# Six attentions of a two-block network: values stationary in two column tiles, outputs split from PSUM, probabilities divided by VectorE before they are transposed

## The reference

```python
# first block, even mixer ("swa"): 8 query heads on 2 key/value heads, window 127, a sink logit a head
p = exp(s - m);  l = sum(p) + exp(sink - m);  o = (p @ v) / l
x = x + concatenate([conv_branch(h), o], -1) @ w_out
# first block, odd mixer ("dil"): 8 heads, three dilated windows merged, so each key counts mult(distance) times
p = mult * exp(s - m);  l = sum(p);  o = (p @ v) / l
x = x + concatenate([o, pool_branch(h)], -1) @ w_out
# second block, twice: "dsa" (4 heads, keys chosen by a top-64 of index scores) and "mla" (4 heads, width 96)
p = softmax(where(allowed, s, NEG));  o = p @ v
merged = sum(gates[n] * (branch[n] @ w_branch[n]));  x = x + merged @ w_out
```

## Time and profile before

| | us |
|---|---|
| median of 3 runs | 1781.18 |
| all runs | 1781.18, 1781.10, 1785.13 |
| the profiled execution | 1784.89 |
| its span in the profile | 1783.1 |
| PE busy | 1768.1 (99%) |
| PE weight loads busy | 1500.8 (84%) |
| DVE busy | 1246.4 (70%) |
| ACT busy | 935.2 (52%) |
| mean granted PE clock, share of full speed | 0.998 |

### The profile page before, as it was taken

How to read it: one execution, slowest core, us unless ns; L and a number is a source line. 1 busy time by engine, 2 the same in 40 slices (tenths; PEclk the granted TensorE clock), 3 DMA queues, 4 the chain that set the end, 5 groups by cost and what they waited for, 6 DMA issues and landing times.

```text
span 1783.1 us, 25102 instructions
## 1 busy us (share of the span) xinstructions
PE 1768.1 (99%) x9850; PEld 1500.8 (84%) x9850; DVE 1246.4 (70%) x1839; ACT 935.2 (52%) x1304; POOL 30.5 (2%) x41
## 2 busy tenths in 40 slices
PE   9999999999999999999999999999999999999998
PEld 8888878888888888888888788888888888888887
DVE  7776645876587657677656977777756878677774
ACT  6554545554455446555545545455544544555553
POOL 0000100000000001000000000000000000000000
PEclk9999999999999999999999999999999999999999
DMA  8666643666666655466656544566666454466663
GB/s 270 199 179 201 179 135 119 191 182 207 184 193 179 201 173 178 121 195 184 195 175 178 173 131 132 179 184 189 190 191 174 143 154 127 149 191 189 188 195 109
DMA packets 231294, 312.26 MB, mean 175 GB/s; under 512 B 23614, under 2 KB 179934, under 8 KB 231178
## 3 DMA queue, kind: packets, MB, share of 16 engines
q1 hardware_dynamic: 231014, 310.35, 57.8%
q10 hardware_dynamic: 164, 0.30, 0.1%
HBM read 308.91 MB, written 1.64 MB: 174 GB/s over the span
## 4 chain that ended last, share of the span: by engine, by line
PE 95%; DVE 3%; ACT 1%; issue 1%; DMA 0%; SPq 0%; POOL 0%; POOLq 0%; ACTq 0%
PE ps L654 26%; PE ps L603 16%; PE ps L605 16%; PE ps L604 16%; PE ps L656 13%; PE ps L1152 1%; PE ps L615 1%; DVE wlo L1734 1%; PE ps L836 1%; PE ps L862 1%; PE ps L849 1%; PE ps L804 1%; DVE m_scr L1743 0%; PE ps L899 0%; DVE m_scr L2383 0%
## 5 line engine op out<-in xcount | busy, mean ns | idle before, releaser
L1734 DVE TENSOR_TENSOR wlo<-staging,whi 128x1024 fp32r<-128x1024 f32 (+1 forms) x580 | 692.5, 1211 | 345.1 <-ACT whi L1250 344.9
L1250 ACT ACTIVATE whi<-staging 128x1024 fp32r<-128x1024 f32 (+1 forms) x580 | 606.4, 1050 | 486.9 <-PE ps L605 305.0
L654 PE MATMUL ps<-hT,whi 128*128 128x512 f32 x1984 | 623.7, 396 | 0.6 <-DVE wlo L1734 0.6
L656 PEld LDWEIGHTS ps<-hT,wlo 128*128 128x128 f32 x1984 | 372.7, 188 | 88.1
L656 PE MATMUL ps<-hT,wlo 128*128 128x256 f32 x1984 | 389.9, 278 | 0.0
L654 PEld LDWEIGHTS ps<-hT,whi 128*128 128x128 f32 x1984 | 302.1, 189 | 0.9 <-DVE wlo L1734 0.8
L603 PE MATMUL ps<-whi,fh 128*128 128x512 f32 x504 | 196.1, 389 | 0.0
L604 PE MATMUL ps<-wlo,fh 128*128 128x512 f32 x504 | 196.1, 389 | 0.0
L605 PE MATMUL ps<-whi,fl 128*128 128x512 f32 x504 | 196.1, 389 | 0.0
L603 PE MATMUL ps<-whi,hT 128*128 128x512 f32 (+3 forms) x464 | 184.5, 398 | 0.8 <-DVE wlo L1734 0.6
L605 PE MATMUL ps<-whi,hT 128*128 128x512 f32 (+3 forms) x464 | 177.4, 382 | 0.0
(11 more groups left out here) (350 smaller groups left out, 1856.4 us busy)
## 6 DMA issues: line engine op xcount, KB each, us to landing
staging<-in_w_in SPq DMA_DIRECT2D x92, 512.0 KB, 3.6
staging<-in_ffn_w_gate SPq DMA_DIRECT2D x84, 512.0 KB, 4.3
staging<-in_ffn_w_up SPq DMA_DIRECT2D x84, 512.0 KB, 4.5
staging<-in_ffn_w_down SPq DMA_DIRECT2D x84, 512.0 KB, 4.1
staging<-in_w_ffn_gate SPq DMA_DIRECT2D x44, 512.0 KB, 4.1
staging<-in_w_ffn_up SPq DMA_DIRECT2D x44, 512.0 KB, 4.5
staging<-in_w_ffn_down SPq DMA_DIRECT2D x44, 512.0 KB, 4.3
staging<-in_od_w_in SPq DMA_DIRECT2D x16, 512.0 KB, 3.6
```

What stands on the lines that cost most here:

```text
L654: e.matmul(o, wh[:, kk, j * 128:j * 128 + 128], hT[:, k, :], start=k == 0, stop=False)
L656: m = e.matmul(o[:, 0:256], wl[:, kk, j * 128:j * 128 + 128], hTh[:, k, :], start=False, stop=k == KD - 1)
L1250: e.activation(high(u)[:, 0:n], stage[u % NS][:, 0:n], ACT.Copy).then_inc(*K.inc("hi", ("hi", u)))
L1734: e.tensor_tensor(low_of(u)[:, 0:n], stage[u % NS][:, 0:n], high(u)[:, 0:n].bitcast(F32), ALU.subtract).then_inc(*K.inc("lo", ("lo", u)))
```

## The change

The groups alternate between the query tiles (`self.groups`: head pair by head pair, tile 0 then tile 1). A value product has the values stationary (128 x 64) and the transposed probabilities streaming (128 x 128); the two heads of a pair write partitions 0 to 63 and 64 to 127, so the output of a pair comes out already transposed, both query tiles in one bank. ACT writes the high part and DVE the low part straight from there; the buffers for the outputs, the output transposes and what followed them go. Since queries now lie along the columns, the division can't be done on the outputs: DVE takes the reciprocal of each group's sums and multiplies the probabilities, before they are transposed. In `swa` the sink's term is made for each group. The pairs of `swa` consist of two heads of different key/value heads, so the rows of `ev_w_out` are loaded in halves to fit.

```diff
             for c in (0, 256):
                 plan_cols(ev, c, 256)
                 plan_cols(ev, 512 + c, 256)
-            for r in (512, 768, 0, 256):
-                plan_rows(A["ev_w_out"][0], [r, r + 128])
+            for r in (512, 576, 640, 704):
+                w = A["ev_w_out"][0]
+                plan.append(([(0, w[r + c:r + c + 64, :], (1, 1024)) for c in (0, 256)], 1024))
+            plan_rows(A["ev_w_out"][0], [0, 128, 256, 384])
...
+                self.late, self.light, self.last = late, light, last
+                self.groups = [(t, h0) for h0 in range(0, H, 2) for t in range(2)]
...
-                self.rows = [(self.mh[:, 4 + k, :], self.ml[:, 4 + k, :], ("swa oT", k // 2))
+                self.rows = [(self.mh[:, 4 + k, :], self.ml[:, 4 + k, :], ("swa oT", k))
...
@@ tensor_program @@
             def attend(a):
...
                         t, h0 = groups[i]
-                        if h0 == 0:
-                            ops[t] = room((P + " o", t))
+                        if t == 0:
+                            ops[h0] = room((P + " o", h0))
                         e.wait_ge(*K.at(P + " pt", i))
-                        for j in range(2):
-                            for kt in range(t + 1):
+                        for kt in range(t + 1):
+                            for j in range(2):
                                 o = (j * (t + 1) + kt) * 128
-                                w = e.matmul(ops[t][:, (h0 + j) * 64:(h0 + j) * 64 + 64], a.pt[i % 2][:, o:o + 128],
-                                             a.vN(kt, h0 + j), start=kt == 0, stop=kt == t)
+                                w = e.matmul(ops[h0][64 * j:64 * j + 64, 128 * t:128 * t + 128], a.vN(kt, h0 + j),
+                                             a.pt[i % 2][:, o:o + 128], start=kt == 0, stop=kt == t)
                         w.then_inc(*K.inc("att", (P + " pv", i)))
-                        if h0 == H - 2:
-                            done(P + " o", t)
+                        if t:
+                            done(P + " o", h0)
...
-                        e.wait_ge(*K.at(P + (" ex" if a.mult is None else " pm"), i))
+                        e.wait_ge(*K.at(P + " light", i))
...
                     e.wait_ge(*K.at("ev k T", 0))
                     yield from attend(m.at)
-                    transposed("swa", m.o, 4)
...
@@ scalar_program @@
             def attend(a):
...
-                        if h0 == H - 2 and a.sink is not None:
-                            l = a.mx[:, 3, 8 * t:8 * t + H]
-                            e.wait_ge(*K.at(P + " sink in", t))
-                            e.activation(l, l, ACT.Exp).then_inc(*K.inc("exp", (P + " sink", t)))
+                        if a.sink is not None:
+                            l = a.mx[:, 3, c0:c0 + 2]
+                            e.wait_ge(*K.at(P + " sink in", i))
+                            e.activation(l, l, ACT.Exp).then_inc(*K.inc("exp", (P + " sink", i)))
+                    if 0 <= turn - 3 < H and groups[turn - 3][0]:
+                        k = groups[turn - 3][1] // 2
+                        hi, _, at = a.out
+                        e.wait_ge(*K.at(P + " pv", turn - 3))
+                        e.activation(hi[:, at + k, :], bk(P + " o", 2 * k)[:, 0:256], ACT.Copy).then_inc(
+                            *K.inc("oT", (P + " oT hi", k)))
...
@@ vector_program @@
             def attend(a, between=lambda turn: None):
...
+                def low(i):
+                    k = groups[i][1] // 2
+                    hi, lo, at = a.out
+                    e.wait_ge(*K.at(P + " oT hi", k))
+                    e.tensor_tensor(lo[:, at + k, :], bk(P + " o", 2 * k)[:, 0:256], hi[:, at + k, :].bitcast(F32),
+                                    ALU.subtract).then_inc(
+                        *K.inc("oTl", (P + " oT", k), ("ev", (P + " o", 2 * k)), *(a.last if i == H - 1 else ())))
+
                 for turn in range(H + 3):
-                    if 0 <= turn - 2 < H and groups[turn - 2][1] == H - 2:
...
+                    if 0 <= turn - 4 and groups[turn - 4][0]:
+                        low(turn - 4)
+                    if 0 <= turn - 1 < H:
                         i = turn - 1
                         t, h0 = groups[i]
                         nk, c0 = 128 * (t + 1), t * 8 + h0
+                        l, r = mx[:, 2, c0:c0 + 2], mx[:, 3, c0:c0 + 2]
+                        p = a.sm[i % 3][:, :, 0:nk]
                         e.wait_ge(*K.at(P + " ex", i))
...
+                        if a.sink is not None:
+                            e.wait_ge(*K.at(P + " sink", i))
+                            e.tensor_tensor(l, l, r, ALU.add).then_inc(*K.inc("att_sum"))
+                            e.wait_ge(*K.now("att_sum"))
+                        e.reciprocal(r, l).then_inc(*K.inc("att_sum", (P + " one by", i)))
+                        if a.light == "dve":
+                            e.wait_ge(*K.now("att_sum"))
+                            e.tensor_tensor(p, p, r.unsqueeze(2).broadcast_to([128, 2, nk]), ALU.mult).then_inc(
+                                *K.inc("light_dve", (P + " light", i)))
                     between(turn)
...
+                low(H - 1)
```

## The result

| | before | after |
|---|---|---|
| median of 4 runs each, us | 1782.96 | 1791.59 |
| all runs | 1781.18, 1781.10, 1785.13, 1784.74 | 1791.60, 1791.58, 1792.67, 1791.22 |
| the profiled execution | 1784.89 | 1791.60 |
| its span | 1783.1 | 1789.8 |

A forecast was written before the change was run, and what follows sets the result against it. PE, busy 99% of the span, bounds the kernel; other engines count only where PE waits. Terms 3.2 + 2.8 + 0.2 - 2.2 = 4.0 us more, giving 1785.2 us from a median of 1781.18; range 1777.5 to 1791.5.

The forecast's parts named there:

- The clock stays at 1.00 outside 268 to 276: Expected sign: granted clock falls only at the stretch already in the old profile (0.50 in 269 to 270).
- rival B: Both mixers: the granted clock falls in a new wait of PE, price 3.3 us, total 1788.5; chance 0.15.
- Odd mixer up to the pool: Divisions of groups 0 to 2 and larger early masks on DVE delay the pool matmuls: 3.2 us lost.
- Odd mixer after the pool: From turn 5 of dil, PE's values wait for DVE's low part in a shared output bank: 2.8 us lost.
- The loop: Dil after the pool: ACT copy and exp, DVE multiplicities, division, mask, low part; 5.3 us from a transpose's end.
- Even mixer: Divisions delay the shifted copies 1.5 us, values gain 1.5, two late waits lose 1.4; stated net 0.2 lost.
- Second mixers: Dsa and mla: transposes gain 1.7, values gain 3.7, shape changes lose 3.2, division covered; net 2.2 us gained.
- the pitch of 0.058: Value products in two column tiles: 0.058 us a record, taken from the convolution's taps, against 0.105 now.
- the change of shape: Switching between column-tiled value products and other matmuls: 0.20 us lost a group, 3.2 in the second mixers.
- Rival A: Value products: column tiles don't overlap, second mixers 3.7 us more, dil and swa about 1; total 1789.9; chance 0.10.
- Rival C: DVE keeps up in dil after the pool, and even-mixer exp doesn't delay copies: 1780.9; chance 0.20.
- rival D: DVE's cover holds everywhere, so PE's savings come through, 4.4 us gained plus about 1: 1775.8; chance 0.10.

The follow-up runs named there:

- e1: Changed kernel without the division (reciprocal and multiply) in dil, the odd mixer's attention: 1786.06 us; odd mixer +1.4 us over the kernel before.
- e4: Kernel before, with only dil's probabilities divided on DVE ahead of their transposes: 1789.06 us; odd mixer +4.6 us.
- e2: Changed kernel with groups in the old order and one output bank per query tile: 1788.15 us, ratio 1.0025 to the kernel before.
- e5: Changed kernel with filler matmuls of zeros on PE ahead of the bank waits in turns 5 and 7 of dil: span 1790.3 us, odd mixer +6.7.
- e7: Changed kernel with the two value matmuls of one head issued back to back: span 1789.2 us; eight value records still 0.59 us.
- e8: Changed kernel with the division's multiply done twice in the second mixers: span 1793.4 us; second mixers +3.2 us over the kernel before.
- e10: e7 with both heads of a pair in one column tile in the second mixers: span 1794.3 us; second mixers +3.2 over the kernel before.
- e11: Changed kernel without reciprocal and division in the second mixers' attentions: span 1789.5 us; second mixers -1.7 us against the kernel before.
- e6: Changed kernel with dil's division multiply on ACT, reciprocal left on DVE: span 1786.7 us; odd mixer +4.2 us over the kernel before.
- e9: Changed kernel with DVE taking dil's low part ahead of the next group's mask: span 1785.2 us; odd mixer +4.8 over the kernel before.

## Why the prediction was right or wrong

**Direction and range** were right, the size short by 2.7 us of 6.7: 1.5 are the fall of the clock in dil, 0.5 the even mixer, 0.5 the second mixers and 0.3 the part ahead of them, less 0.1 in the rest of the odd mixer. The step that failed is the one on the clock, "The clock stays at 1.00 outside 268 to 276"; the sum had nothing for a fall. A fall in a new wait of PE stood as rival B with a chance of 0.15 and a price of 3.3. That B's time, 1788.5, nearly is the 1788.7 measured is luck, since the fall cost half of that price and the rest came from elsewhere.

**Odd mixer up to the pool.** Right: 3.2 forecast, 3.0 measured. Of its parts the divisions were 1.9 to 2.0 rather than 2.4 (e1, e4) and the larger early groups 1.1 rather than 0.8 (e1, and 1.0 in e2). The transposes of group 1 stood at 706.83, 705.9 plus the 1.0 of the shift.

**Odd mixer after the pool.** 2.8 forecast, 4.4 measured, and 2.9 once the fall's 1.5 are taken off. The loop was laid out well: turn 5 at 721.51 (forecast 720.9 and 1.0 of shift), turn 7 at 729.72 (729.1 and 1.0), both behind DVE's low part. Turn 10 came at 740.67 where 738.2 and 1.0 were due, 1.5 late: the fall lies between. The wait for the bank is one place where DVE's lateness appears; e4 and e2 show that without it the same time goes at the division.

**The clock.** It fell once in dil in all six kernels that keep the changed order with the division on DVE as it stands (the changed one, e5, e7, e8, e10, e11), at 708, 722, 723 or 730, and in e2; never in e1, e4, e6, e9, nor where dil is as before. Each fall in dil began within 2 us of the end of a wait of PE for DVE. I had priced it at 3.3, from a stretch which by its loss (3.4) was as long as two of these, and against it I held the one wait of 1.84 us before the taps, which left the clock up. That was one sample, and e4 has the other: its even mixer is that of the kernel before, PE waits 2.31 us at the same place, the clock reads 0.73 in 252 to 253 and 0.50 behind it, and the taps take 4.48 us rather than 2.80:

```profile
251.82 4.48 PE L899 MATMUL ps<-ev_u,ev_w 128*32 128x256 f32 x48 [2.31 <-DMA ev_u<-ev_shift]
```

With the new `swa` it is the same: e5 and e7 lost 1.7 within 247 to 251, behind waits of 1.6 and 0.6 us that the changed kernel has too, without a fall there. What decides which wait brings it down is open: e6 has waits of 1.8 and 1.5 us in dil, e9 of 1.9 and 1.5, and neither a fall. That waits are needed for it is supported, and not shown, by e1 and e4, whose waits in dil are at most 1.3 us and which have no fall there, one trace each; e5 doesn't add to it.

**Even mixer.** 0.2 forecast, +0.7 measured, within -2 to +3. The 0.2 isn't what the prediction's own terms give: 1.5 for the copies and 1.4 for two waits, less 1.5 gained, are 1.4. Of the parts, the gate multiply came at 242.25 rather than 240.10, and the taps at 252.32 rather than 250.84, 1.5 later or 1.2 from the start of the stage. The waits for the low part's bank and the convolution's sums in the last turns were 0.37 and 0.49 us rather than 1.4, and the larger new waits stand ahead of the taps: 1.60 for the division and 0.56 for a low part, which use up the old wait for the copies (1.84 before, 0.17 now). From one kernel to another the stage moves by 1.0 to 1.7 us with a fall more or less, so the half microsecond isn't to be explained.

**Second mixers.** 2.2 forecast, 1.7 measured, and the terms close. Removed transposes: 16 x 0.109 = 1.7. Values: 8 x (0.84 - 0.59) + 8 x (0.39 - 0.37) = 2.2. What follows them: 16 x 0.14 = 2.2 lost, 12 times at transposes and 4 times at the first product behind the last group. In my terms: the pitch of 0.058 was right (0.055), and what goes with a group, 0.05 and 0.20, was 0.29 (0.15 ahead, in a four-record group of 0.37 = 0.15 + 4 x 0.055, and 0.14 behind). The term that was mis-sized is the change of shape, by 0.04 a group, 0.6 in all. So the column tiles by themselves gave nothing here; what was gained is the output transposes that they made needless. The 0.14 doesn't come from the overlap: with one column tile (e10) the transposes take 0.59 all the same.

Rival A is excluded by e10: without overlap the second mixers would be 4.9 us longer. By the rule of the Trainium skill (TensorE: Matmul & The Clock Gate, Part 3, What overlaps and what doesn't), a weight load runs beside matmuls in flight only when the row group differs, and both tiles here have the same rows. The traces disagree, and the measurement decides: a record costs 0.11 us in one tile, as much as its stream alone, and 0.055 in two, so load and stream of one tile run beside those of the other. The same page of the Trainium skill (Part 3, Measured speedup vs the span model) gives a speedup of 2.38 for three column tiles; two tiles here gave 1.02/0.59 = 1.7, which agrees in kind. Rival C is refuted, since DVE didn't keep up (3.8 us of bank waits, 3.3 for the division). So is rival D: its cover doesn't hold in the odd mixer, while it does in the second mixers.

## What to carry to other kernels

- A division moved from the outputs to the probabilities is cheap only where the engine that does it is early: the same kind of instructions cost nothing in the second mixers and 4.5 us in the odd one, 6.0 with the fall of the clock that came with them. Read it stage by stage from the windows of that engine, and look for what it must finish next.
- A wait that stands at a buffer may belong to the queue behind it. Taking the buffer away moved the wait to the division (e2); taking work off the queue shortened it (e1: 2.4 rather than 3.8 us at the bank).
- New waits of PE of 1 to 2 us in a stretch of small matmuls should be charged for the clock with more than a small chance. In the odd mixer a fall cost 0.8 to 1.5 us, depending on where it lay.

## What the runs showed of the hardware

- Falls of the granted clock take away 1.7 us each, in even and odd mixer alike, and the sums in every kernel are 0, 1.7, 3.4 or 5.1. Less than that reaches the end where PE waits for others behind the fall: 1.5 us in the changed kernel, 1.4 in e7, 0.8 in e5. The place differs between kernels whose code there is the same (722, 723 or 730), so a single trace doesn't say which wait is safe.
- Two column tiles of 64 run beside each other even if each tile's two matmuls are issued back to back (0.59 us for eight records in either order, 1.02 in one tile).
- A group of column-tiled matmuls makes the untiled transposes or product behind it 0.14 us later, with one tile in use or two, and has 0.15 us of its own beside its records; with four records in a group, two tiles gain next to nothing over the old form (0.37 against 0.39).
